# Two adaLN buffers become ring slots 15 and 16 of a fixed cycle, and the first eight expert picks are added amid the query chunks

## The reference, cut to what matters

```python
mod = silu(c) @ ada_w[l] + ada_b[l]              # 6 x 1024 numbers: shift1, scale1, gate1, shift2, scale2, gate2
h = rms_norm(x, norm1_g[l]) * (1 + scale1) + shift1
proj = h @ w_in[l]                               # q, k, v of two attentions, two gates
y_a = sliding_window_attention(rope(q_a), rope(k_a), v_a, sinks)
y_b = stick_breaking_attention(q_b, k_b, v_b)
merged = sigmoid(g_a) * (y_a @ w_branch_swa[l]) + sigmoid(g_b) * (y_b @ w_branch_sb[l])
x = x + gate1 * (merged @ w_out[l])
h2 = rms_norm(x, norm2_g[l]) * (1 + scale2) + shift2
q = h2 @ peer_wq[l]                              # 8 heads x 2 x 128
# per head: top 16 of each half's 128 sub-key scores, top 16 of their 256 sums -> 128 experts per token
x = x + gate2 * sum over the 128 picks of  gate * gelu(peer_u[expert] . h2) * peer_v[expert]
```

## Time and profile before

| | us |
|---|---|
| median of 3 runs (lowest, highest) | 1830.06 (1828.57, 1831.49) |
| the profiled execution: its time | 1828.28 |
| its span in the trace | 1826.5 |
| PE, DVE, ACT, POOL busy | 1497.6, 1348.8, 577.4, 508.5 |
| DMA in the span | 665.35 MB, mean 364 GB/s |
| DMA in 118 to 185 (the later steps): busy share of 16 engines, rate | 0.74, 253 GB/s |

### The profile page before, as it was taken

The page is one execution under the profiler, slowest core; times in us unless marked ns, Lnnn a source line. Parts: engine busy times, 40 slices in busy tenths (PEclk is TensorE's granted clock), DMA queues, the critical chain, the costliest instruction groups (busy, mean ns, idle before and its releaser), DMA issues.

```text
span 1826.5 us, 18012 instructions
## 1 busy us (share of the span) xinstructions
PE 1497.6 (82%) x6060; PEld 894.8 (49%) x6060; DVE 1348.8 (74%) x3178; ACT 577.4 (32%) x1282; POOL 508.5 (28%) x556
## 2 busy tenths in 40 slices
PE   3999999877778787877889999997877878787886
PEld 2888986333333233333378988932333333333333
DVE  7887999767676777665568886887777676777554
ACT  3465453222121223222245654432121222221222
POOL 0000023433333333333200000253433333333340
PEclk8999999998899999899999999999999998899998
DMA  9877869999999999999957754899999999999994
GB/s 376 282 248 248 282 260 395 422 421 421 421 421 422 421 421 422 421 421 421 405 204 266 248 198 136 336 400 421 422 421 421 421 421 421 421 421 422 421 422 175
DMA packets 102909, 665.35 MB, mean 364 GB/s; under 512 B 11809, under 2 KB 11937, under 8 KB 31649
## 3 DMA queue, kind: packets, MB, share of 16 engines
q0 software_dynamic: 79488, 578.85, 77.3%
q1 hardware_dynamic: 23328, 85.35, 13.4%
HBM read 663.11 MB, written 1.05 MB: 364 GB/s over the span
## 4 chain that ended last, share of the span: by engine, by line
DMA 48%; PE 30%; DVE 16%; ACT 4%; issue 2%; SPq 0%; DVEq 0%; ACTq 0%
DMA big<-pairs,big 30%; DMA late<-pairs,big 17%; PE yac L662 12%; PE acc L428 10%; PE pg L428 3%; DVE big L1121 2%; DVE big L974 2%; DVE wsp L407 2%; PE acc L547 1%; DVE late L1121 1%; ACT big L819 1%; DMA big<-ada 1%; ACT wsp L399 1%; DVE big L1040 1%; ACT big L773 1%
## 5 line engine op out<-in xcount | busy, mean ns | idle before, releaser
L662 PE MATMUL yac<-big 128*128 128x512 f32 x1184 | 564.9, 631 | 129.8 <-ACT big L819 129.8
L662 PE MATMUL yac<-late,big 128*128 128x512 f32 x864 | 430.8, 653 | 121.3 <-ACT big L819 121.3
L662 PEld LDWEIGHTS yac<-big 128*128 128x128 f32 x1184 | 232.3, 201 | 455.3 <-issue 269.7
L1314 POOL DMA_INDIRECT big<-pairs,big x296 | 283.9, 959 | 504.9 <-PE yac L662 390.2
L662 PEld LDWEIGHTS yac<-late,big 128*128 128x128 f32 x864 | 175.2, 208 | 373.7 <-issue 206.3
L1314 POOL DMA_INDIRECT late<-pairs,big x216 | 203.0, 940 | 381.6 <-PE yac L662 328.0
L428 PE MATMUL acc<-hs,wsp 128*128 128x256 f32 x2208 | 285.1, 288 | 6.0 <-ACT big L763 6.0
L428 PEld LDWEIGHTS acc<-hs,wsp 128*128 128x128 f32 x2208 | 272.6, 194 | 11.6 <-ACT big L763 8.6
L1121 DVE CUSTOM_DVE_ANT_0 big<-big,acc 128x1024 f32<-128x1024 f32 x148 | 179.0, 1220 | 111.4 <-DMA big<-pairs,big 111.1
L810 ACT ACTIVATE big<-big 128x4 f32<-128x4 f32 (+1 forms) x138 | 28.3, 205 | 709.9 <-DVE big L1121 709.9
L819 ACT ACTIVATE big<-con,big 128x128 f32<-128x128 f32 x512 | 164.7, 390 | 247.9 <-DVE big L1136 247.4
(11 more groups left out here) (135 smaller groups left out, 1067.8 us busy)
## 6 DMA issues: line engine op xcount, KB each, us to landing
raw<-stream SPq DMA_DIRECT2D x136, 512.0 KB, 4.5
big<-ada_pairs POOLq DMA_DIRECT2D x40, 1024.0 KB, 7.5
big<-ada SPq DMA_DIRECT2D x16, 512.0 KB, 13.3
big<-pairs,big POOLq DMA_INDIRECT x296, 21.4
late<-pairs,big POOLq DMA_INDIRECT x216, 21.6
big<-subkeys SPq DMA_DIRECT2D x2, 1024.0 KB, 11.8
x<-xT SPq DMA_DIRECT2D x1, 1024.0 KB, 10.1
outT<-big SPq DMA_DIRECT2D x1, 1024.0 KB, 3.9
```

Of the source, the lines that this page charges most:

```text
L662: mm = pe.matmul(yac[:, 2 * t + w, :], diag(n), row(n)[:, D + w * 512:D + (w + 1) * 512], start=(n % (SLOTS // TT) == 0), stop=(n % (SLOTS ...
L1314: g.indirect_dma_start(row(n), None, pairs, bass.IndirectOffsetOnAxis(ap=col(Q_IDX + n).bitcast(U32), axis=0)).then_inc(row_in[n % RING], 16)
```

## The change

The diff is cut to its core; the lines left out are counters and the assertion. Terms: `ADA_FIRST` lists the head steps m that reduce a column (m = 7 and 9 lie behind a rotation), `ADA_STEPS` the 24 steps, with 9, 11, 13, 15, 16, 17 twice and 21 to 23 no more, `TOPK_WQ` triples of (query chunk, unit, part). The ring has 16 slots: 0 to 7 as before, 8 and 9 in the four adaLN buffers, 10 to 15 in the place of the former 8 to 13. `SLOT_OF` gives a pick's slot and `USES` a slot's picks; picks 0 to 9 take slots 0 to 9, picks 10 to 13 slots 0 to 3 again, picks 14 and 15 slots 10 and 11, picks 16 to 19 slots 4 to 7. A gather waits for the pick before it in its slot; a slot's reuse is 16 picks later in the steady part, and 13 or 14 for a few early uses of slots 10 and 11.

```diff
 N_ADA, N_ADA1 = 48, 16
 N_ADA2 = N_ADA - N_ADA1
-ADA_HEADS = N_QA + N_PAD
-ADA_STEPS = tuple(range(24))
-ADA_BR = (1, 3, 5)
+ADA_FIRST = (0, 1, 2, 3, 4, 7, 9, 10, 11)
+ADA_HEADS = len(ADA_FIRST)
+ADA_STEPS = tuple(sorted(tuple(range(21)) + (9, 11, 13, 15, 16, 17)))
+ADA_BR = (1, 3, 5, 7)
...
-ADA_WQ = (0, 0, 4, 5, 10, 11)
-TOPK_WQ = ((1, 0, 0), (2, 0, 1), (3, 0, 2), (3, 0, 3), (6, 1, 0), (7, 1, 1), (8, 1, 2), (9, 1, 3),
-           (12, 2, 0), (12, 2, 1), (13, 2, 2), (13, 2, 3))
+TOPK_WQ = ((1, 0, 0), (1, 0, 1), (2, 0, 2), (2, 0, 3), (4, 1, 0), (4, 1, 1), (5, 1, 2), (6, 1, 3),
+           (9, 2, 0), (9, 2, 1), (11, 2, 2), (11, 2, 3))
+DOTS_WQ = (8, 10)
+GATES_WQ = (9, 11)
+GELU_WQ = (9, 11)
+DIAG_WQ = (10, 12)
+PICKS_WQ = (11, 13)
...
-RING = 14
+RING = 16
 LATE = 6
 RING_BIG = RING - LATE
+RING_LOW = 8
+CYCLE = [0, 1, 2, 3, 10, 11, 4, 5, 6, 7, 12, 13, 14, 15, 8, 9]
+SLOT_OF = list(range(RING_BIG)) + [r for n, r in sorted(
+    (RING_BIG + CYCLE.index(r) + RING * t - (2 * min(t, 4) if r in (10, 11) else 0), r)
+    for r in range(RING) for t in range(SLOTS // RING + 2))][:SLOTS - RING_BIG]
+USES = [[n for n in range(SLOTS) if SLOT_OF[n] == r] for r in range(RING)]
...
-            r = n % RING
+            r = SLOT_OF[n]
+            if r < RING_LOW:
+                return col(r * ROW, ROW)
             if r < RING_BIG:
-                return col(r * ROW, ROW)
+                return col(B_ADA + (r - RING_LOW) * ROW, ROW)
             return late[:, r - RING_BIG, :]
...
                     if c == 7:
                         h2_by_tokens(0)
+                    for g, step in enumerate(PICKS_WQ):
+                        if step == c:
+                            for n in range(*GROUP_OF[g]):
+                                add_pick(L, n)
                 head_subkeys(L, 7)
                 pe.wait_ge(acc_free, nth(L, EVACS, EVACS + 2))
                 h2_by_tokens(1)
-                for n in range(SLOTS):
+                for n in range(GROUP_OF[len(PICKS_WQ)][0], SLOTS):
...
+                    for g, step in enumerate(GELU_WQ):
+                        if step == c:
+                            pick_gelu(L, g)
+                    for g, step in enumerate(DIAG_WQ):
+                        if step == c:
+                            pick_diag(L, g)
                 store_subkeys(L, 7)
                 for g in range(GROUPS):
-                    pick_gelu(L, g)
-                    pick_diag(L, g)
+                    if g >= len(DIAG_WQ):
+                        pick_gelu(L, g)
+                        pick_diag(L, g)
...
-                        act.wait_ge(slot_done, nth(L, SLOTS, SLOTS - 8))
+                        act.wait_ge(slot_done, nth(L, SLOTS, USES[RING_BIG + 1][-1] + 1))
...
                 for m in range(M_QB):
                     dve_low(dve, L, m + AHEAD)
-                    if m < N_QA:
-                        ada_next(L, m)
-                    elif m < M_PAD:
+                    if M_V <= m < M_PAD:
                         rope(L, m - M_V)
-                    else:
-                        ada_next(L, N_QA + m - M_PAD)
+                    if m in ADA_FIRST:
+                        ada_next(L, ADA_FIRST.index(m))
...
-                    if s in ADA_STEPS:
-                        ada_next(L, ADA_HEADS + ADA_STEPS.index(s))
+                    for n, step in enumerate(ADA_STEPS):
+                        if step == s:
+                            ada_next(L, ADA_HEADS + n)
                     if s % 2 == 0 and 0 <= (s - 2) // 2 < PAIRS:
                         pair_d2(L, (s - 2) // 2)
...
-                dve.wait_ge(ada_free, nth(L, N_ADA, 24))
-                d.link(v.tensor_tensor(mod[:, N_ADA1:40], mod[:, N_ADA1:40], par[:, N_ADA1:40], ALU.add))
+                dve.wait_ge(ada_free, nth(L, N_ADA, N_ADA2))
+                d.link(v.tensor_tensor(mod[:, N_ADA1:48], mod[:, N_ADA1:48], par[:, N_ADA1:48], ALU.add))
...
                     dve_low(dve, L, M_OUT + c + AHEAD)
-                    ada_next(L, ADA_OUT + c)
+                    if c < N_OUT - 1:
+                        ada_next(L, ADA_OUT + c)
                     chunk_used(dve, L, M_OUT + c)
                     xc = x[:, c * T:(c + 1) * T]
                     v.scalar_tensor_tensor(xc, pg[:, c % 2, 0:T], mod[:, 16 + c:17 + c],
                                            xc, ALU.mult, ALU.add).then_inc(pg_free, 1)
+                    if c == N_OUT - 1:
+                        ada_next(L, ADA_OUT + c)
                 source(L, 3, 1)
...
-                    for n, step in enumerate(ADA_WQ):
+                    if c == DOTS_WQ[0]:
+                        unit_gates(L, 0)
+                    for g, step in enumerate(DOTS_WQ):
                         if step == c:
-                            ada_next(L, N_ADA - len(ADA_WQ) + n)
+                            pick_dots(L, g)
+                    for g, step in enumerate(GATES_WQ):
+                        if step == c:
+                            pick_weights(L, g)
...
-                    unit_gates(L, u)
+                    if u:
+                        unit_gates(L, u)
                     for q, g in enumerate(g for g in range(GROUPS) if GROUP_OF[g][0] // PICKS == u):
-                        pick_dots(L, g)
+                        if g >= len(DOTS_WQ):
+                            pick_dots(L, g)
...
                     n = L * N_ADA + a
                     if n >= SA:
                         pool.wait_ge(ada_free, n - SA + AP)
+                    if L and a < SA:
+
+                        pool.wait_ge(slot_done, (L - 1) * SLOTS + USES[RING_LOW + a // AP][-1] + 1)
...
-                    if RING_BIG <= n < RING_BIG + W:
-
-                        pool.wait_ge(chunk_done, (L + 1) * SPLITS + n - RING_BIG + 1)
-                    if n == RING_BIG + W:
+                    r = SLOT_OF[n]
+                    before = USES[r].index(n) - 1
+                    if before >= 0:
+                        pool.wait_ge(slot_done, L * SLOTS + USES[r][before] + 1)
+                    elif RING_LOW <= r < RING_BIG:
+
+                        pool.wait_ge(ada_free, L * N_ADA + ada_columns(L))
+                    elif RING_BIG <= r < RING_BIG + W:
+
+                        pool.wait_ge(chunk_done, (L + 1) * SPLITS + r - RING_BIG + 1)
+                    elif r >= RING_BIG + W:
 
                         pool.wait_ge(h2tok_done, L * TT + TT)
-                    if n >= RING:
-                        pool.wait_ge(slot_done, L * SLOTS + n - RING + 1)
```

More of the change, by code:

```diff
@@ L80 @@
 M_WQ = M_OUT + N_OUT
-assert ADA_OUT + N_OUT + len(ADA_WQ) == N_ADA
+assert ADA_OUT + N_OUT == N_ADA and ADA_HEADS + len(ADA_STEPS) >= N_ADA - N_ADA1
 assert N_QA == N_V and SPLITS % RAW == 0 and M_G % W == 0
@@ L131 @@
 HB = HALF * T
-B_QP = RING_BIG * ROW
+B_QP = RING_LOW * ROW
 QP = 4
@@ L380, in rows_landed @@
         def rows_landed(eng, L, n):
-            per_layer = len(range(n % RING, SLOTS, RING))
-            eng.wait_ge(row_in[n % RING], nth(L, per_layer * 16, (n // RING + 1) * 16))
+            uses = USES[SLOT_OF[n]]
+            eng.wait_ge(row_in[SLOT_OF[n]], nth(L, len(uses) * 16, (uses.index(n) + 1) * 16))
         def token_half(tensor, t, k0=0, k1=KD):
@@ L1248, in _ @@
                 dve.wait_ge(ada_free, nth(L, N_ADA, ada_columns(L)))
-                d.link(v.tensor_tensor(mod[:, 40:48], mod[:, 40:48], par[:, 40:48], ALU.add))
                 d.clear()
                 for u in range(UNITS):
-                    unit_gates(L, u)
+                    if u:
+                        unit_gates(L, u)
                     for q, g in enumerate(g for g in range(GROUPS) if GROUP_OF[g][0] // PICKS == u):
-                        pick_dots(L, g)
+                        if g >= len(DOTS_WQ):
+                            pick_dots(L, g)
                         if u + LOOK < UNITS:
@@ L1259, in _ @@
                             topk_part(L, u + LOOK, q)
-                        pick_weights(L, g)
+                        if g >= len(GATES_WQ):
+                            pick_weights(L, g)
                         if g == EARLY // GROUP + 2:
@@ L1304, in gather @@
                 def gather(n):
-                    if RING_BIG <= n < RING_BIG + W:
-                        pool.wait_ge(chunk_done, (L + 1) * SPLITS + n - RING_BIG + 1)
-                    if n == RING_BIG + W:
+                    r = SLOT_OF[n]
[7 more added lines that the diff above has]
+                    elif r >= RING_BIG + W:
                         pool.wait_ge(h2tok_done, L * TT + TT)
-                    if n >= RING:
-                        pool.wait_ge(slot_done, L * SLOTS + n - RING + 1)
                     g.indirect_dma_start(row(n), None, pairs,
                                          bass.IndirectOffsetOnAxis(ap=col(Q_IDX + n).bitcast(U32), axis=0)).then_inc(
-                        row_in[n % RING], 16)
+                        row_in[SLOT_OF[n]], 16)
                 for n in range(SLOTS):
```

## The result

The changed kernel takes 1836.36 us in the median of 7 runs (1833.93 to 1838.40), the kernel before 1829.67 beside it (7 runs, 1828.57 to 1831.51): a ratio of 1.0032 on record, interval 1.0022 to 1.0042 (the two medians alone give 1.0037). So it is slower by 6 to 7 us, 4.9 us above the forecast of 1831.5 and inside the range. "Within 0.2%" (0.49) didn't come, "slower by over 0.2%" (0.27) did. The two profiled executions have spans of 1826.5 and 1832.1, 5.6 apart.

| stage | forecast, both layers | layer 1 | layer 2 | sum |
|---|---|---|---|---|
| start to first norm | 0 | +0.2 | | +0.2 |
| heads (norm to the start of the steps) | +2.3 | +2.1 | +1.2 | +3.2 |
| steps, to BR | +7.2 | +3.0 | +4.8 | +7.8 |
| BR and OUT, to the second norm | -0.4 | +3.6 | -0.5 | +3.1 |
| second norm to first gather | -2.3 | -1.1 | -0.4 | -1.5 |

The account below looks back on a forecast made before the run. DMA engines bound the retrieval, PE, DVE and ACT in turn the other stages. Terms -2.3 + 2.5 - 7.8 + 2.3 + 7.2 - 0.4 = +1.5 on the profiled 1828.28, plus 1.8 for the median: 1831.5 us, range 1824.5 to 1838.

Parts of the forecast that it names:

- B: Slower rival, chance 0.11: denser adaLN loads at the doubled steps get slower, some 3.5 us more a layer, 1838.5.
- D: Slower rival, chance 0.09: in the query stage DVE's first dots wait for rows sharing DMA; some 5 us, 1836.5.
- Gathers earlier: Before the first gather: one low part fewer ahead of it, 1.15 us a layer, -2.3 us in all.
- No idle at the hand-over: Query stage into retrieval: ten gathers and early picks keep DMA busy, -7.8 us; raw chunk loads after the first gather, +2.5.
- Rival C: Slower rival, chance 0.06: the DMA idle at the hand-over isn't recoverable, so the 7.8 us stays, 1839.3.
- Dots and adds amid the query chunks: Query stage: eight early picks' work on DVE and 7.4 us on PE is moved and hidden by DMA; cost 0.
- The column at m = 9: Heads: a column between the last rotation and a low part delays the first pair by 1.14 us a layer, +2.3.
- The doubled steps: Steps with two columns: PE waits 0.4 us, then 3.2 at pair 7 behind column 30's late load; +7.2 both layers.
- Column 20: Column in step 10: its load lands 0.9 us later than wanted, making PE wait 0.4 us for `pair_d2`.
- Rival A: Faster rival, chance 0.21: in the steps the adaLN lag never reaches PE, so 7.2 us falls away, 1824.3.
- BR, OUT, the rest: BR and OUT: first layer +1.0 for BR's last column, -1.1 for OUT's last; second layer -0.3; sum -0.4 us.
- The turn from one layer to the next, and the end: Last dot to next norm or end: layer 2's first adaLN pairs and the copy wait for later picks, cost 0.

Follow-up runs that it names:

- e4: The kernel before with only the changed kernel's column places (ring of 14, top-k and picks as before): 1842.01 us, ratio 1.0068.
- e5: The changed kernel with 14 slots in a cycle and columns nearly as before, keeping early picks and the changed top-k: 1823.46 us, ratio 0.9963.
- e9: e5 with the top-k's parts put back at the query chunks of the kernel before: 1829.80 us, ratio 1.0003.
- e8: The kernel before with one unused DVE product of 1.14 us more in BR's last chunk, both layers: 1832.81 us, ratio 1.0014.
- e2: The changed kernel with `pair_d2` ahead of a doubled step's second column: 1828.92 us, ratio 0.9997.
- e3: The changed kernel with BR's last column moved behind OUT's last residual: 1835.95 us, ratio 1.0029.
- e6: The changed kernel with 16 unused PE transposes between BR and OUT: 1834.46 us, ratio 1.0025.
- e1: The changed kernel with the head column of m = 9 moved to m = 8: 1833.38 us, ratio 1.0018.

## Why the prediction was right, and where it was off

The mechanism was right: a gain at the hand-over, paid for and more by the columns; e4 and e5 show the two halves each alone. The size was less so: +1.5 us forecast, +6.7 measured by the medians. The range held the result because its upper end of 1838 had been set for the rivals B and D, and neither came; what used up that room in the profiled run was in good part the clock, 2.7 us at OUT and some 1.5 in the steps, which no term had. To that extent the hit is luck. In its steps:

*Gathers earlier*, -2.3: measured -1.5, -1.08 in the first layer (forecast 1.15), -0.44 in the second, where the first 32 matmuls behind the norm took 6.42 us against 5.72.

*No idle at the hand-over*, -7.8 + 2.5: the dip is gone and the stage is 0.8 and 3.5 us shorter (forecast 1.5 and 3.9). Rival C is refuted by the share of 1.02 and D by the same window; e9 shows how near D was. e5 against before gives 6.2 us for this half and e4 against after 5.7 to 6.6, forecast 7.6.

*Dots and adds amid the query chunks*, 0: the cost is hidden as forecast, with 420 GB/s or more over 300 to 320, but its size was misread. Four picks took PE 7.03 us, 1.76 us a pick and not 0.93, so the eight took 14 us and not 7.4, and PE came to pick 8 at 320.55, 58 us behind the first gather and not 50.

*The column at m = 9*, +2.3: PE's wait grew from 1.05 to 2.19 in the first layer, 1.14, as worked out, and to 1.77, 0.72, in the second. The heads grew by 2.1 and 1.2. In the first layer 0.9 of that is the first products behind the norm, 6.30 us against 5.38, with a clock of 0.50 in them. That is not the column's: e5 and e8, whose head columns stand as in the kernel before, have heads 0.8 us longer than the profiled run before in the first layer and 1.0 in the second, with a wait of 1.05.

*The doubled steps*, +7.2: +7.8. Column 20 came with a wait of 0.62 as against 0.9. The load of columns 30 and 31 went out at 149.0 instead of 147.2, took 6.5 us instead of 7.0, and PE waited 2.47 instead of 3.2; in the second layer 2.89. What is left in the second layer, some 1.5, I put down to the clock, 0.57 over 1054 to 1058; that is not tested by itself. Rival A is refuted by these waits. B is refuted by the landings: the nine loads issued from 110 to 170 took 5.6 to 8.0 us, median 6.5, where the seven of the kernel before took 5.9 to 7.7, median 7.4. The two that PE came to wait for took 6.5 and 7.5. By the fit of the Trainium skill ("DMA: Bandwidth & Descriptors", Anatomy of one DMA) an estimate for such a pair is 4.4 us. The trace disagrees: 6.5 here, and 5.0 at the least in the steps of either layer.

*BR, OUT, the rest*, -0.4: this is the term that was mis-sized; it measured +3.1. Its +1.0 for the last BR column was right as a wait (1.73 to 2.83). What the sum lacked for this execution was that behind this wait PE ran at half its clock: OUT's 192 matmuls took 25.99 us instead of 23.33, +2.7. In e2 and e4, with the same wait, they took 23.3, and the two layers of the stage came to +0.3 together, near the -0.4. How often the clock falls there is open; e3 and e6, which take the wait away, moved the median by 0.4 and 1.9. And the -1.1 for the last OUT column did not come. The residual itself is no longer late: at 226.53 DVE was behind the earlier trace rows, now it waits for PE. But the path to the norm runs over PE's sixteen matmuls behind OUT, which took 3.62 us in both kernels. ACT waits for them now; before, its own chain behind the residual ended within 0.2 us of them. From the start of the sixteen to the reciprocal it was 4.3 us and is 4.2. DVE, PE and ACT of the kernel after:

```profile
234.17 0.48 DVE L1258 SCALAR_TENSOR_TENSOR x<-pg,big,x 128x256 f32<-128x256 f32 x1 [0.46 <-PE pg L441]
...
233.97 3.62 PE L514 MATMUL yac<-big,con 128*128 128x256 f32 x16
...
237.62 0.47 ACT L763 ACTIVATE big<-yac,con 128x256 f32<-128x256 f32 x1 [1.22 <-PE yac L514]
```

I had read a late instruction of DVE as the path without looking at what the norm's end waited for.

*The turn from one layer to the next, and the end*, 0: -1.3 and -1.4. The same sixteen matmuls took 3.54 us at a clock of 0.64 before and 2.19 at 1.00 after, PE's rows of before and after:

```profile
922.32 3.54 PE L512 MATMUL yac<-big,con 128*128 128x128 f32 x16 [1.44 <-ACT big L923]
```

```profile
929.27 2.19 PE L525 MATMUL yac<-big,con 128*128 128x128 f32 x16 [1.44 <-ACT big L947]
```

At the end they took 3.68 before and 2.19 after. The change has no part in it: e4 and e8, whose code is that of the kernel before from the retrieval on, have 2.19 at the end too, and the same turn as the kernel after. It is the profiled run before that was slow there. This says how far one profiled run can be read: the clock gave and took up to 2.7 us in single places, for reasons that the edits don't set alone. So it is no surprise that the medians are 6.7 apart and the spans 5.6. By the medians e4 puts the columns' price at 11.9, where the forecast's three terms make 2.3 + 7.2 - 0.4 = 9.1. The 2.8 between have the size of the clock's falls and of the 1.1 that didn't come; the runs don't split them further.

## What to carry to other kernels

Before storage is freed by moving work, check that the storage is what is short: here early consumption and an earlier first request filled the gap with 14 slots, and two more were worth nothing. Work moved to an engine that is a step behind is priced at the next wait of the engine that it feeds, and the order within the step (what PE waits for first, the filler second) can be worth a large part of it: 7.4 us of some 12 here. Where a change makes a wait of PE longer, widen the range by the clock behind it: here 1.1 us of wait came with 2.7 of slower matmuls in one execution, and with none in two others. And read an experiment by its median before its profile: in e3 and e8 the profile spoke for the theory, and the median came nearer the rival's time.

## What the runs showed of the hardware

PE's clock after a wait was the surprise. At OUT's start an idle of 1.73 us was followed by clock 1.00 in every profile. After longer idles there the clock fell in four of six cases: 2.83 us in the kernel after (0.50 over the next 4 us) and in e1 (0.58), 2.69 and 2.28 in e8 (0.57 both times), but not after 2.84 in e2 and in e4 (1.00, which is 33 matmuls in 4 us again). Elsewhere it is as mixed: in the steps' second layer it fell after 2.89 us in the kernel after and after 4.19 in e1, in their first layer it stayed at 1.00 after 2.61 in e3 and 3.56 in e4, and in e9 it was 0.66 over 280 to 290 around an idle of 4.68. So the length of the idle alone doesn't decide.

What a fall cost can be worked out at OUT's start alone: its 192 matmuls took 23.3 us at full clock, 24.8 in e1 and e8, and 26.0 in the kernel after. What decides between the two outcomes stays open. The profiled run of e8 shows that a longer wait of PE can come with a fall without any of the change.

The other finding is the queue of gathers: with 16 slots instead of 14 each took 26.3 us instead of 21.2 to 22.0 to land, and the rate stayed at 421 GB/s.
